# Two transformer blocks on one core: three pads and one moved tile change where the tiles of the on-chip memory begin

## The chip, the core and the metric

The kernel runs on one core of a Trainium2 chip. The metric is device time in microseconds for one execution. The kernel before took 1553.38 us, the median of three runs (1552.86 to 1556.38). One further execution was profiled; its own time stands in the table below.

The engines are TensorE (PE; its weight loads are listed apart as PEld), VectorE (DVE), ScalarE (ACT), GpSimd (POOL) and SyncE (SP, which issues nearly all transfers here). They share one on-chip memory of 128 partitions. A tile takes the same range of byte addresses in each partition, so a tile is placed by one number, its byte offset within a partition.

## The reference

Everything is float32, with 512 tokens and a model width of 1024. Cut to what matters:

```
first_block(x):
  u = rmsnorm(h); u_ssm, q, k, v = split(u @ w_in)              # 1024 -> 2048
  y_ssm  = s5_branch(u_ssm)                                     # 32 groups, state 64, gelu, glu
  y_attn = stick_breaking_attention(q, k, v)                    # 8 heads of 64
  gates  = sigmoid(u @ w_gate + b_gate)                         # 1024 -> 2048
  h += (g_ssm * (y_ssm @ w_up_ssm) + g_attn * (y_attn @ w_up_attn)) @ w_out
  h += relu(rmsnorm(h) @ w_ff1)**2 @ w_ff2                      # 1024 -> 4096 -> 1024
  return rmsnorm(h)
second_block(x, p):
  h += gla_mixer(rms_norm(h))          # gated linear attention, 4 heads, chunks of 64 tokens
  h += (p[0] @ ple_proj[0]) * sigmoid(rms_norm(h) @ ple_gate[0])
  h += fox_mixer(rms_norm(h))          # causal softmax attention with forget gates, 16 heads of 64
  h += (p[1] @ ple_proj[1]) * sigmoid(rms_norm(h) @ ple_gate[1])
  return rms_norm(h)
```

## The kernel before, in words

Activations stand with the features on the partitions and the 512 tokens along the free axis; `h` has 8 such chunks. Weights come as 105 units of 128 x 2048 floats (1 MB). SP loads a unit into one of two slots of `wraw`. ACT copies it, rounded, into `whi` (line 1044) and DVE writes the rest, `wraw - whi`, into `wlo` (line 1596). The activations are split in the same way: `uhi`/`ulo` (the normalised input), `yhi`/`ylo` and `ahi`/`alo` (the outputs of the two branches), `mhi`/`mlo` (the merged branches), `hdhi`/`hdlo` (the squared hidden layer), `pehi`/`pelo` (the `p` input).

The helper `three` (lines 498 to 500) makes each product from three matmuls, high x high, low x high and high x low. The profile names the operand that streams through the array (the moving one) first and the one that is loaded as weights (the stationary one) second: `ps<-uhi,whi` streams 512 columns of `uhi` past a 128 x 128 block of `whi`.

```
def three(out, lh, ll, rh, rl_, start, stop=False, done=None):
    nc.tensor.matmul(out, lh, rh, start=start, stop=False, skip_group_check=True)
    nc.tensor.matmul(out, lh, rl_, start=False, stop=False, skip_group_check=True)
    mm = nc.tensor.matmul(out, ll, rh, start=False, stop=stop, skip_group_check=True)
```

The stages, in the order of the program, with the stretch of the trace in which each lies:

- 0 to 264 us: first norm, then four rounds of `mixer`, each an S5 group and two heads of stick-breaking attention, with parts of the `w_in` products put between them. Small fp32 matmuls and transposes read `ident`, `ET`, `uch`, `Es`, `U4`, `M`, `H`, `X`; the attention reads `qs`, `kh`, `kl`, `athi`, `atlo`, `vhi`, `vlo`.
- 264 to 440 us: `merge`: the glu and the two up-projections (`y` and `a` tiles), the gates (`u`), and the output product (`m`).
- 440 to 800 us: `ff`, eight times: 96 matmuls on `u` (first layer), then 96 on `hd` (second layer), all with 512 columns.
- 800 to 1042 us: `gla_head` four times (its values are made with the weights streaming, `ps<-whi,uhi 128x256`), gates, output product.
- 1042 to 1150 us: `p[0]` product (`pe` tiles), its gate on `u`, norm.
- 1150 to 1430 us: `fox`, eight times two heads: scores from `fka`, `fkb`, `fq`, transposes of `pr`, values from `pthi`, `ptlo`, `fvhi`, `fvlo`, with `u` products between.
- 1430 to 1557 us: output product, `p[1]` product, gate, last norm.

The order of the work is written out by hand on each engine and is held by semaphores. No scheduler and no pool stands behind it. Tiles are placed by the stack of scopes at the head of `build` (lines 125 to 280): `sb` takes the next free bytes, rounded up to 32, and leaving a scope gives them back. So the offset of a tile is the sum of what stands before it. `vecs` has 97 floats (388 bytes, 416 with rounding), and `ident`, the tile behind it, therefore begins at a remainder of 32 when its offset is divided by 512.

These are the remainders modulo 512 of the tiles' offsets in the two built programs. Nearly every tile that TensorE reads has a length that is a multiple of 512 bytes, so the blocks within a tile mostly keep its remainder. Of the tiles near the top of the memory, `mlo` begins at byte 210784 before, `pthi` at 215936.

| tiles that TensorE reads | where read | before | after |
|---|---|---|---|
| `whi`, `wlo`, `uhi`, `ulo` | everywhere | 128 | 128 |
| `ident`, `ones`, `headones`, `identr`, `trir`, masks | norms, transposes, attention | 32 | 128 |
| `uch`, `vT`, `ET`, `H`, `Es`, `M`, `X`, `U4`, `tT` | S5, as fp32 | 96 | 128 |
| `qs`, `kh`, `kl`, `athi`, `atlo`, `vhi`, `vlo` | first attention | 96 | 128 |
| `acc`, `pp`, `pehi`, `pelo` | norms, `p` products | 96 | 128 |
| `yhi`, `ylo`, `ahi`, `alo`, `mhi`, `mlo` | merge | 352 | 128 |
| `hdhi`, `hdlo` | feed-forward | 352 | 128 |
| GLA tiles (`gr`, `kdec`, `qzhi`, `kihi`, `gvhi`, `aihi`, `sthi`, ...) | GLA | 352 | 128 |
| fox tiles (`fq`, `fka`, `fkb`, `fvhi`, `pr`, `pthi`, `ptlo`, ...) | fox | 384 | 128 |
| `rstd` (one column, broadcast) | norms | 128 | 224 |
| `wa2` | GLA, 8 matmuls | 224 | 320 |

Of the kernel before, what the change touches and what calls it, by code (L numbers as in the profile page):

```python
# [25 lines left out]
P = 128  # L26
# [9 lines left out]
GLA_N = 8  # L36
# [85 lines left out]
def build(nc, wstream, xT, pT, vecs_d, cst_d, s5p_d, wa2_d, outT):  # L122
    ctx = ExitStack()
    with ctx:
# [11 lines left out]
        whi = sb("whi", [P, 2, UW], F32R)  # L136
        wlo = sb("wlo", [P, 2, UW], F32R)
        vecs = sb("vecs", [P, NVEC])
        ident = sb("ident", [P, P])
        ones = sb("ones", [P, P])  # L140
        headones = sb("headones", [P, P])
# [19 lines left out]

        wa2 = sb("wa2", [16, T])
        s5r = sb("s5r", [P, 2, S5_PAIRS], F32R)

        with scope() as m:
            ys = sb("ys", [P, HC, T], F32, m)
            ya = sb("ya", [P, HC, T], F32, m)
            with scope() as e:
                blockpos = sb("blockpos", [P, NB], F32, e)
                s5p = sb("s5p", [P, 24, S5_PAIRS], F32, e)  # L170
                s5w = sb("s5w", [P, 5, 2, 2, S5_PAIRS], F32, e)
                s5b = sb("s5b", [P, 4, 512], F32, e)
                uch = sb("uch", [P, L, NB], F32, e)
                vT = sb("vT", [P, T], F32, e)
                ET = sb("ET", [P, 2, QP, L, 32], F32, e)
                H = sb("H", [P, 2, QP, L + 1, 32], F32, e)
                decay = sb("decay", [P, QP, NB], F32, e)
                with scope() as s:
                    sq = sb("sq", [P, 2, T], F32, s)
                    un = sb("un", [P, 2, T], F32, s)  # L180
                    acc = sb("acc", [P, T], F32, s)
                    with scope() as pl:
                        pe_in = sb("pe_in", [P, 2, T], F32, pl)
                        pehi = sb("pehi", [P, 2, T], F32R, pl)
                        pelo = sb("pelo", [P, 2, T], F32R, pl)
                        pp = sb("pp", [P, DC, T], F32, pl)
                        sg = sb("sg", [P, 2, T], F32, pl)

                    sq2, acc2 = un, pp[:, 6, :]
                    cst_in = sb("cst_in", [P, 5, P], F32, s)  # L190
                with scope() as s:
                    qs = sb("qs", [P, 2, T], F32R, s)
                    kh = sb("kh", [P, 2, T], F32R, s)
                    atlo = sb("atlo", [P, NZ], F32R, s)
                    vhi = sb("vhi", [P, TT, P], F32R, s)
                    vlo = sb("vlo", [P, TT, P], F32R, s)
                    att = sb("att", [P, NZ], F32, s)
                    athi = sb("athi", [P, NZ], F32R, s)
                    Es = sb("Es", [P, 2, 512], F32, s)
                    kl = sb("kl", [P, 2, T], F32R, s)  # L200
                    tmp = sb("tmp", [P, QP, L + 1, 32], F32, s)
                    M = sb("M", [P, QP, P], F32, s)
                    cosT = sb("cosT", [P, QP, NB], F32, s)
                    sinT = sb("sinT", [P, QP, NB], F32, s)
                    rin = sb("rin", [P, 2, QP, NB], F32, s)
                    zst = sb("zst", [P, 2, QP, NB], F32, s)
                    X = sb("X", [P, 2, QP, NB], F32, s)
                    U4 = sb("U4", [P, QP, NB], F32, s)
                    tT = sb("tT", [P, QP, P], F32, s)
                    gl = Es  # L210
            with scope() as s:
                yhi = sb("yhi", [P, HC, T], F32R, s)
                ylo = sb("ylo", [P, HC, T], F32R, s)
                ahi = sb("ahi", [P, HC, T], F32R, s)
                alo = sb("alo", [P, HC, T], F32R, s)
                gate = sb("gate", [P, 2, 4, T], F32, s)
                glu = sb("glu", [P, 2, T], F32, s)
                mg = glu
                mhi = sb("mhi", [P, DC, T], F32R, s)
                mlo = sb("mlo", [P, DC, T], F32R, s)  # L220
# [5 lines left out]
        with scope() as m:  # L226
            og = sb("og", [P, DC, T], F32, m)
            gr = sb("gr", [P, DC, T], F32, m)
            with scope() as s:
                alr = sb("alr", [P, T], F32, s)  # L230
                cum = sb("cum", [P, GLA_H, T], F32, s)
                eq = sb("eq", [P, T], F32, s)
                ek = sb("ek", [P, T], F32, s)
                kd = sb("kd", [P, T], F32, s)
                qin = sb("qin", [P, T], F32, s)
                kin = sb("kin", [P, T], F32, s)
                kdec = sb("kdec", [P, T], F32, s)

                qzhi = sb("qzhi", [P, TT, 4, GLA_C], F32R, s)
                qzlo = sb("qzlo", [P, TT, 4, GLA_C], F32R, s)  # L240
                kihi = sb("kihi", [P, T], F32R, s)
                kilo = sb("kilo", [P, T], F32R, s)
                kdhi = sb("kdhi", [P, T], F32R, s)
                kdlo = sb("kdlo", [P, T], F32R, s)
                gvhi = sb("gvhi", [P, TT, 256], F32R, s)
                gvlo = sb("gvlo", [P, TT, 256], F32R, s)
                ai = sb("ai", [P, TT, P], F32, s)
                aihi = sb("aihi", [P, TT, P], F32R, s)
                ailo = sb("ailo", [P, TT, P], F32R, s)
                st = sb("st", [P, 2, 256], F32, s)  # L250
                sthi = sb("sthi", [P, GLA_N, 256], F32R, s)
                stlo = sb("stlo", [P, GLA_N, 256], F32R, s)

                otm = gr[:, 4:6, :].rearrange("p a t -> p (a t)").rearrange("p (t c) -> p t c", c=256)
                gsq = gr[:, 6, 0:256]
                gss, g_half, g_t, g_y = (sb(n, [P, TT], F32, s) for n in ("gss", "g_half", "g_t", "g_y"))
            with scope() as s:
                fl = sb("fl", [16, 3, T], F32, s)
                nchi = sb("nchi", [16, T], F32R, s)
                nclo = sb("nclo", [16, T], F32R, s)  # L260
                gq8 = sb("gq8", [P, 1], F32, s)
                qk = sb("qk", [P, 2, T], F32, s)
                qksq = sb("qksq", [P, 2, T], F32, s)
                f_t = sb("f_t", [P, 2, T], F32, s)
                f_half = sb("f_half", [P, 2, T], F32, s)
                f_y = sb("f_y", [P, 2, T], F32, s)
                fq = sb("fq", [P, 2, 2, T], F32R, s)
                fka = sb("fka", [P, 2, T], F32R, s)
                fkb = sb("fkb", [P, 2, T], F32R, s)
                fvT = sb("fvT", [P, T], F32, s)  # L270
                fvhi = sb("fvhi", [P, TT, P], F32R, s)
                fvlo = sb("fvlo", [P, TT, P], F32R, s)
                pr = sb("pr", [P, NZ], F32, s)
                pthi = sb("pthi", [P, NZ], F32R, s)
                ptlo = sb("ptlo", [P, NZ], F32R, s)
                nmax = sb("nmax", [P, TT], F32, s)
                rsum = sb("rsum", [P, TT], F32, s)
                rinv = sb("rinv", [P, TT], F32, s)
        ps = ctx.enter_context(nc.psum_tensor("ps", [P, 8, 512], F32))
        flat = ps[:, :, :].rearrange("p b n -> p (b n)")  # L280

# [213 lines left out]
        def _(pe):  # L495
# [326 lines left out]
            def gla_head(i, last=False):  # L822
# [28 lines left out]
                for t in range(TT):  # L851
                    out = ps[:, 6 + t // 2, (t % 2) * 256:(t % 2) * 256 + 256]
                    three(out, aihi[:, t, :], ailo[:, t, :], gvhi[:, t, :], gvlo[:, t, :], True)
                    for v in range(2):
                        c = 2 * t + v
                        if c == 0:
                            continue
                        pe.wait_ge(st_ready, i * (GLA_N - 1) + c)
                        half = [q[:, t, 2 * v:2 * v + 2, :].rearrange("p a b -> p (a b)") for q in (qzhi, qzlo)]
                        three(out, *half, sthi[:, c, :], stlo[:, c, :], False, v == 1, go_mm if v == 1 and t % 2 else None)  # L860

                if not last:
                    gla_values(i + 1)
# [175 lines left out]
        def _(act):  # L1039
# [300 lines left out]
            def gla_head(i, last=False):  # L1340
# [6 lines left out]
                copy(aihi[:, :, :], ai[:, :, :]).then_inc(ai_hi, 1)  # L1347
                for c in range(GLA_N - 1):
                    act.wait_ge(st_done, i * (GLA_N - 1) + (c + 1))
                    copy(sthi[:, c + 1, :], st[:, c % 2, :]).then_inc(st_hi, 1)  # L1350
                if not last:
                    split_hi(None, U_GLA % 2, i + (U_GLA + 4) // 2, i * 4 + (DONE[U_GLA] + 6))

# [236 lines left out]
        def _(dve):  # L1590
# [435 lines left out]
            def gla_head(i, last=False):  # L2026
# [12 lines left out]
                for c in range(NS):  # L2039
# [7 lines left out]
                        V.scalar_tensor_tensor(st[:, c % 2, :], st[:, (c - 1) % 2, :], eq[:, at:at + 1], kv, ALU.mult,  # L2047
                                               ALU.add).then_inc(st_done, 1)
                    dve.wait_ge(st_hi, i * NS + (c + 1))
                    V.tensor_tensor(stlo[:, c + 1, :], st[:, c % 2, :], sthi[:, c + 1, :], ALU.subtract).then_inc(st_ready, 1)  # L2050
                    dve.wait_ge(st_ready, i * NS + (c + 1))
                split_lo(i * 2 + (U_GLA + 3), (U_GLA + 3) % 2)
                if not last:
# [375 lines left out]
```

## Time and profile before

| | |
|---|---|
| median of three runs | 1553.38 us |
| the profiled execution | 1558.66 us, of which the span from first to last instruction is 1556.9 us |
| mean granted TensorE clock | 0.963 of full speed |
| PE busy | 1433.3 us (92%) in 6912 matmuls |
| DVE busy, ACT busy, POOL busy | 949.2, 712.2, 81.8 us |
| DMA | 118.16 MB, 76 GB/s on average |
| chain that ended last | PE 68%, DVE 16%, ACT 11%, issue 5% |

How to read it: matmuls are pipelined, so the length of one record (about 0.4 us for 512 columns) is not what one costs. What a matmul costs in a dense row of them is the distance from its start to the next one's start. The rows of the timeline give starts to a hundredth of a microsecond, so that distance is taken over many matmuls: the difference of two starts, divided by how many matmuls lie between. In a run of `three` the lines 498, 499 and 500 repeat in that order, three matmuls for each line 499.

### The profile page before, as it was taken

Reading aid. Unit: us, or ns where it says so; the run is one execution under the profiler, and the core shown is the slowest. Engines: PE = TensorE matmul, PEld = TensorE weight load, DVE = VectorE, ACT = ScalarE, POOL = GpSimd, SP = SyncE. Lnnn points to the kernel's source line nnn. Section 1 sums busy time; section 2 is a strip of 40 time slices with the busy share of each in tenths; the row PEclk is TensorE's granted clock in tenths of the full one; section 3 lists DMA queues with packets and bytes.
Section 4 is the critical chain, followed back from the end, with each engine's and each line's share of the span. In section 5 each row is a group of like instructions: output and inputs, shape, how many; then the busy total and the mean of one; then the engine's idle time right before and its main releaser. Section 6 shows DMA issues by size and latency. Waiting matters only on the chain.

```text
span 1556.9 us, 18015 instructions
## 1 busy us (share of the span) xinstructions
PE 1433.3 (92%) x6912; PEld 1193.2 (77%) x6912; DVE 949.2 (61%) x1324; ACT 712.2 (46%) x940; POOL 81.8 (5%) x81
## 2 busy tenths in 40 slices
PE   4798889999989999999979999999789999996996
PEld 3687777788868888888868898787667777775875
DVE  6798776444354444444479676536776667777365
ACT  4577767332232222222246443334375666556251
POOL 3000000000200000000020000031100000000202
PEclk9999999999989999999989999999799999996998
DMA  5111011322212322222321122223121111111211
GB/s 188 55 54 55 1 55 54 109 90 99 98 65 81 108 84 104 90 99 81 108 82 55 54 85 76 96 81 109 55 81 54 54 54 54 54 54 68 81 55 54
DMA packets 19237, 118.16 MB, mean 76 GB/s; under 512 B 2400, under 2 KB 3680, under 8 KB 5616
## 3 DMA queue, kind: packets, MB, share of 16 engines
q1 hardware_dynamic: 18896, 116.38, 20.9%
q0 software_dynamic: 288, 1.05, 0.2%
q8 instruction: 37, 0.61, 0.2%
q14 instruction: 16, 0.13, 0.0%
HBM read 115.32 MB, written 2.10 MB: 75 GB/s over the span
## 4 chain that ended last, share of the span: by engine, by line
PE 68%; DVE 16%; ACT 11%; issue 5%; DVEq 0%; DMA 0%; ACTq 0%
PE ps L498 21%; PE ps L499 20%; PE ps L500 20%; DVE wlo L1596 1%; PE ps L681 1%; ACT whi L1044 1%; PE ps L951 1%; ACT fq L1044 1%; ACT fka L1044 1%; PE ps L562 1%; DVE att L1841 1%; DVE nmax L2164 1%; DVE acc L374 1%; ACT pthi L1044 1%; ACT att L1163 1%
## 5 line engine op out<-in xcount | busy, mean ns | idle before, releaser
L498 PE MATMUL ps<-uhi,whi 128*128 128x512 f32 x1168 | 469.2, 402 | 12.7 <-DVE ulo L1645 5.9
L499 PE MATMUL ps<-ulo,whi 128*128 128x512 f32 x1168 | 460.0, 394 | 0.0
L500 PE MATMUL ps<-uhi,wlo 128*128 128x512 f32 x1168 | 459.6, 393 | 0.0
L1596 DVE TENSOR_TENSOR wlo<-wraw,whi 128x2048 fp32r<-128x2048 f32 x105 | 240.2, 2290 | 109.8 <-ACT whi L1044 108.3
L1044 ACT ACTIVATE whi<-wraw 128x2048 fp32r<-128x2048 f32 x105 | 200.3, 1908 | 189.2 <-PE ps L500 189.0
L498 PEld LDWEIGHTS ps<-uhi,whi 128*128 128x128 f32 x1168 | 222.7, 191 | 66.5 <-issue 16.3
L500 PEld LDWEIGHTS ps<-uhi,wlo 128*128 128x128 f32 x1168 | 222.4, 190 | 47.8
L499 PEld LDWEIGHTS ps<-ulo,whi 128*128 128x128 f32 x1168 | 223.0, 191 | 45.9 <-issue 1.9
L498 PE MATMUL ps<-hdhi,whi 128*128 128x512 f32 x256 | 101.3, 396 | 0.0
L499 PE MATMUL ps<-hdlo,whi 128*128 128x512 f32 x256 | 101.3, 396 | 0.0
L500 PE MATMUL ps<-hdhi,wlo 128*128 128x512 f32 x256 | 101.2, 396 | 0.0
L1960 DVE TENSOR_TENSOR h<-ps,h 128x512 f32<-128x512 f32 x64 | 44.1, 690 | 54.7 <-PE ps L500 54.5
L1952 DVE TENSOR_TENSOR hd<-rl 128x512 f32<-128x512 f32 x32 | 22.0, 690 | 86.3 <-ACT rl L1287 86.3
L1287 ACT ACTIVATE rl<-ps 128x512 f32<-128x512 f32 x32 | 19.2, 599 | 118.0 <-PE ps L500 117.3
L2186 DVE TENSOR_TENSOR ptlo<-ps,pthi 128x1280 fp32r<-128x1280 f32 x16 | 23.9, 1491 | 63.8 <-ACT pthi L1044 63.8
L500 PEld LDWEIGHTS ps<-hdhi,wlo 128*128 128x128 f32 x256 | 48.1, 188 | 11.7
L499 PEld LDWEIGHTS ps<-hdlo,whi 128*128 128x128 f32 x256 | 48.1, 188 | 11.6
L498 PEld LDWEIGHTS ps<-hdhi,whi 128*128 128x128 f32 x256 | 48.1, 188 | 11.6
L1934 DVE TENSOR_TENSOR h<-ps,h 128x512 f32<-128x512 f32 x24 | 16.6, 691 | 65.0 <-PE ps L500 65.0
L1044 ACT ACTIVATE uhi<-un 128x512 fp32r<-128x512 f32 x48 | 30.1, 632 | 52.9 <-DVE un L1652 52.5
L1065 ACT ACTIVATE sq<-h 128x512 f32<-128x512 f32 x56 | 33.2, 621 | 41.6 <-DVE h L1934 24.2
L1480 ACT ACTIVATE pr<-ps,nmax 128x512 f32<-128x512 f32 (+1 forms) x64 | 32.9, 527 | 39.6 <-DVE nmax L2164 39.6
(391 smaller groups left out, 2371.5 us busy)
## 6 DMA issues: line engine op xcount, KB each, us to landing
wraw<-wstream SPq DMA_DIRECT2D x105, 1024.0 KB, 4.7
h<-xT SPq DMA_DIRECT2D x4, 512.0 KB, 5.6
outT<-pp SPq DMA_DIRECT2D x8, 256.0 KB, 2.1
s5b<-s5p_d SPq DMA_DIRECT2D x1, 1024.0 KB, 11.8
pe_in<-pT POOLq DMA_DIRECT2D x2, 512.0 KB, 3.7
cst_in<-cst_d SPq DMA_DIRECT2D x5, 64.0 KB, 10.1
reset<-cst_d SPq DMA_DIRECT2D x1, 256.0 KB, 11.1
ones<-cst_d SPq DMA_DIRECT2D x1, 64.0 KB, 2.2
```

The source lines that it names most:

```text
L498: nc.tensor.matmul(out, lh, rh, start=start, stop=False, skip_group_check=True)
L499: nc.tensor.matmul(out, lh, rl_, start=False, stop=False, skip_group_check=True)
L500: mm = nc.tensor.matmul(out, ll, rh, start=False, stop=stop, skip_group_check=True)
L1044: return A(out, in_, ACT.Copy, scale=scale)
L1065: A(sq[:, c % 2, :], h[:, c, :], ACT.Square).then_inc(sq_done, 1)
L1287: A(rl[:, m % 2, :], ps[:, a + m, :], ACT.Relu).then_inc(rl_done, 1)
L1480: e = A(pr[:, at], zf[:, at], ACT.Exp, bias=nmax[:, col], accum_out=rsum[:, col])
L1596: V.tensor_tensor(wlo[:, slot, :], wraw[:, slot, :], whi[:, slot, :], ALU.subtract).then_inc(lo_done, 1)
L1934: V.tensor_tensor(h[:, m, :], ps[:, banks[b] + k, :], h[:, m, :], ALU.add).then_inc(h_added, 1)
L1952: V.tensor_tensor(hd[:, m % 2, :], rl[:, m % 2, :], rl[:, m % 2, :], ALU.mult).then_inc(hd_done, 1)
L1960: V.tensor_tensor(h[:, m, :], ps[:, bank, :], h[:, m, :], ALU.add).then_inc(h_added, 1)
L2186: V.tensor_tensor(ptlo[:, :], tf, pthi[:, :], ALU.subtract).then_inc(pt_ready, 1)
```

## The change

It touches the placement of tiles, and for two of them the size. Two tiles named `pad0` (96 bytes) and `pad1` (192 bytes) are put in, which nothing reads or writes. `s5w` (1280 bytes, used by POOL and DVE in the set-up of the S5 part) moves from the scope `e` to the end of the scope behind `tT`. `gq8` (4 bytes, a factor used by DVE) moves to the end of its scope. `sthi` and `stlo` lose their first block of 256 columns, which no instruction used, and the indices into them go down by one. "Three pads" of the change's title are these two and the room that `gq8` took as one.

No instruction is added, removed or moved on any engine: the order of both programs is the same on PE, DVE, ACT, POOL and SP, and so are all semaphores, waits and transfers. Only addresses differ. `rstd` and `wa2` are read by TensorE and do not end up at 128 (table above).

```diff
         vecs = sb("vecs", [P, NVEC])
+        sb("pad0", [P, 24])
         ident = sb("ident", [P, P])
...
         s5r = sb("s5r", [P, 2, S5_PAIRS], F32R)
+        sb("pad1", [P, 48])
...
                 s5p = sb("s5p", [P, 24, S5_PAIRS], F32, e)
-                s5w = sb("s5w", [P, 5, 2, 2, S5_PAIRS], F32, e)
                 s5b = sb("s5b", [P, 4, 512], F32, e)
...
                     tT = sb("tT", [P, QP, P], F32, s)
+                    s5w = sb("s5w", [P, 5, 2, 2, S5_PAIRS], F32, s)
...
-                sthi = sb("sthi", [P, GLA_N, 256], F32R, s)
-                stlo = sb("stlo", [P, GLA_N, 256], F32R, s)
+                sthi = sb("sthi", [P, GLA_N - 1, 256], F32R, s)
+                stlo = sb("stlo", [P, GLA_N - 1, 256], F32R, s)
...
-                gq8 = sb("gq8", [P, 1], F32, s)
                 qk = sb("qk", [P, 2, T], F32, s)
...
                 rinv = sb("rinv", [P, TT], F32, s)
+                gq8 = sb("gq8", [P, 1], F32, s)
```

## Rows read from the trace of the kernel before

**Rows 1.** The page: chain that ended last, share of the span by engine.

```profile
PE 68%; DVE 16%; ACT 11%; issue 5%; DVEq 0%; DMA 0%; ACTq 0%
```

**Rows 2.** Busy time by stretch (us), four stretches; after PEclk the DMA share.

```profile
464.00:800.00 336.00, 334.65 (x1453) 272.52 (x1452) 154.62 (x158) 96.88 (x103) 6.16 (x5) 1.00 0.27 97
...
264.00:440.00 176.00, 170.13 (x736) 138.54 (x736) 73.14 (x82) 56.69 (x60) 11.94 (x6) 0.98 0.26 90
440.00:464.00 24.00, 21.68 (x86) 17.58 (x86) 16.77 (x23) 9.70 (x14) 0.00 (x0) 0.84 0.15 47
```

**Rows 3.** Timeline of PE, `hd` matmuls: start us, us, instruction.

```profile
688.64 0.40 PE L499 MATMUL ps<-hdlo,whi 128*128 128x512 f32 x1
...
709.64 0.40 PE L499 MATMUL ps<-hdlo,whi 128*128 128x512 f32 x1
```

**Rows 4.** Timeline of PE, the `u` matmuls behind them.

```profile
710.11 0.39 PE L498 MATMUL ps<-uhi,whi 128*128 128x512 f32 x1
...
711.72 0.39 PE L499 MATMUL ps<-ulo,whi 128*128 128x512 f32 x1
...
731.44 0.39 PE L499 MATMUL ps<-ulo,whi 128*128 128x512 f32 x1
```

**Rows 5.** Timeline of PE, the `m` and the `pe` matmuls.

```profile
387.11 0.40 PE L499 MATMUL ps<-mlo,whi 128*128 128x512 f32 x1
...
431.21 0.40 PE L499 MATMUL ps<-mlo,whi 128*128 128x512 f32 x1
...
1042.54 0.40 PE L499 MATMUL ps<-pelo,whi 128*128 128x512 f32 x1
...
1046.04 0.40 PE L499 MATMUL ps<-pelo,whi 128*128 128x512 f32 x1
```

**Rows 6.** Timeline of PE in fox and mixer: `u`, then value matmuls.

```profile
1200.29 0.39 PE L499 MATMUL ps<-ulo,whi 128*128 128x512 f32 x1
...
1205.55 0.39 PE L498 MATMUL ps<-pthi,fvhi 128*128 128x512 f32 x1
...
1206.23 0.33 PE L498 MATMUL ps<-pthi,fvhi 128*128 128x384 f32 x1
...
81.74 0.39 PE L498 MATMUL ps<-athi,vhi 128*128 128x512 f32 x1
...
82.43 0.34 PE L498 MATMUL ps<-athi,vhi 128*128 128x384 f32 x1
```

**Rows 7.** Groups by line and shape: matmuls; busy us, mean ns, idle before.

```profile
L498 PE MATMUL ps<-hdhi,whi 128*128 128x512 f32 x256 | 101.3, 396 | 0.0
...
L500 PE MATMUL ps<-mhi,wlo 128*128 128x512 f32 x64 | 25.3, 396 | 0.0
...
L498 PE MATMUL ps<-yhi,whi 128*128 128x512 f32 x48 | 19.1, 399 | 2.5 <-DVE ylo L1889 1.6 <-issue 0.8
...
L498 PE MATMUL ps<-pehi,whi 128*128 128x512 f32 x32 | 13.0, 406 | 0.0
...
L498 PE MATMUL ps<-ahi,whi 128*128 128x512 f32 x32 | 12.7, 396 | 0.0
...
L620 PE MATMUL ps<-U,Es 128*128 128x128 f32 x64 | 7.8, 275 | 0.0
```

**Rows 8.** Groups by line and shape: DVE and ACT on `u` and `hd` tiles.

```profile
L1645 DVE TENSOR_TENSOR ulo<-un,uhi 128x512 fp32r<-128x512 f32 x48 | 33.3, 693 | 3.5 <-ACT uhi L1044 2.8
...
L1956 DVE TENSOR_TENSOR hdlo<-hd,hdhi 128x512 fp32r<-128x512 f32 x32 | 20.7, 689 | 26.0 <-ACT hdhi L1044 26.0
```

**Rows 9.** Timeline of PE: 16 S5 matmuls, 8 transposes, and the start of `ff`.

```profile
65.85 1.95 PE L620 MATMUL ps<-U,Es 128*128 128x128 f32 x16
...
879.35 1.03 PE L870 MATMUL ps<-ident,gr 128*128 128x128 f32 x8
...
443.26 0.63 PE L499 MATMUL ps<-ulo,whi 128*128 128x512 f32 x1
443.69 0.63 PE L500 MATMUL ps<-uhi,wlo 128*128 128x512 f32 x1
```

More of the change, by code:

```diff
@@ L859, in gla_head @@
                         half = [q[:, t, 2 * v:2 * v + 2, :].rearrange("p a b -> p (a b)") for q in (qzhi, qzlo)]
-                        three(out, *half, sthi[:, c, :], stlo[:, c, :], False, v == 1, go_mm if v == 1 and t % 2 else None)
+                        three(out, *half, sthi[:, c - 1, :], stlo[:, c - 1, :], False, v == 1, go_mm if v == 1 and t % 2 else None)
                 if not last:
@@ L1349, in gla_head @@
                     act.wait_ge(st_done, i * (GLA_N - 1) + (c + 1))
-                    copy(sthi[:, c + 1, :], st[:, c % 2, :]).then_inc(st_hi, 1)
+                    copy(sthi[:, c, :], st[:, c % 2, :]).then_inc(st_hi, 1)
                 if not last:
@@ L2049, in gla_head @@
                     dve.wait_ge(st_hi, i * NS + (c + 1))
-                    V.tensor_tensor(stlo[:, c + 1, :], st[:, c % 2, :], sthi[:, c + 1, :], ALU.subtract).then_inc(st_ready, 1)
+                    V.tensor_tensor(stlo[:, c, :], st[:, c % 2, :], sthi[:, c, :], ALU.subtract).then_inc(st_ready, 1)
                     dve.wait_ge(st_ready, i * NS + (c + 1))
```

## The prediction

> **What bounds the kernel now.** I read the page first: PE carries 68% of the chain that ended last, DVE 16% of it and ACT 11% [rows 1]. Then the busy time by stretch: over the feed-forward stage, 464 to 800 us, PE is busy for 334.65 of 336.00 us while DVE is at 154.62 and ACT at 96.88; from 264 to 440 us it is 170.13 of 176.00 [rows 2]. So in those stretches the time is the number of matmuls times what one costs in a dense row, and nothing else.
>
> The change moves no instruction and no wait. It can act only through what an access costs at another address. So I then read, on the timeline, the distance between the starts of neighbouring matmuls of one shape (512 columns, full clock), family by family, and set it beside the table of offsets:
>
> - moving tile at 128, weights at 128 (`u` on `whi`): from 711.72 to 731.44 us lie 87 matmuls, so 19.72 / 87 = 226.7 ns each [rows 4].
> - moving tile at 352, weights at 128 (`hd`): from 688.64 to 709.64 us lie 90 matmuls, so 21.00 / 90 = 233.3 ns [rows 3]. The `m` tiles, also at 352: 44.10 / 189 = 233.3 ns. The `pe` tiles, at 96: 3.50 / 15 = 233.3 ns [rows 5]. The `y` and `a` tiles are at 352 too; I take the same for them.
> - both at 384 (`pthi` on `fvhi`): 0.68 / 3 = 226.7 ns. Both at 96 (`athi` on `vhi`): 0.69 / 3 = 230 ns, three matmuls only [rows 6].
>
> So the cheaper spacing goes with 128 and 384, the dearer one with 96 or 352, or with operands that differ. These data do not separate "both operands at one remainder" from "each on a multiple of 64 bytes" (128 and 384 are, 96 and 352 are not), and they need not: after the change all these tiles are at 128, which satisfies both. Other causes I looked for do not fit. `m` has `u`'s shape, 8 chunks, and still costs 233.3; `pthi` lies as high in the memory as `mlo` and costs 226.7; `hd` and `u` alternate in one stage beside the same DVE, ACT and DMA work.
>
> **The change, part by part.** Each row family that goes from 233.3 to 226.7 ns gains 6.67 ns a matmul. The counts are three times those of one line in the groups [rows 7].
>
> - `hd`: 3 x 256 = 768 matmuls x 6.67 ns = 5.1 us. All on the path: PE never stops there, and DVE and ACT are idle for half of the stage and more [rows 2].
> - `m`: 3 x 64 = 192, 1.3 us. On the path: a dense row, and the norm behind it waits for its last block.
> - `y` and `a`: 3 x (48 + 32) = 240, 1.6 us. On the path by the same stretch of 264 to 440 us, where PE is idle for 5.9 us in all.
> - `pe`: 3 x 32 = 96, 0.6 us. They stand in program order ahead of the matmuls that spread the norm, so I count them whole. If DVE's norm scale came later than they end, up to 0.6 us would be hidden.
>
> Together 1296 matmuls and 8.6 us. The rest is small or unknown:
>
> - Starts of a row. Behind `hd`, the first seven spacings of `u` take 1.61 us, 230 ns each, before 226.7 sets in [rows 4]: 0.02 us. With one remainder everywhere I expect this to go at the 8 passages of the feed-forward stage, 0.2 us. In fox, 23 spacings from 1200.29 to 1205.55 us average 228.7 ns [rows 6], 0.05 us above 226.7; there are about 48 such short rows of 24 in fox and mixer, 2.2 us if all of it went. But these start behind shorter matmuls, whose lengths do not change, and fox's tiles (384) already have the cheap spacing. Nearest to the first kind, I take 0.4 us in all, bounds 0 and 2.4.
> - Matmuls of 128 columns. Sixteen of S5 (`U`, `Es`, both at 96) take 1.95 us, of which the last record is 0.275 [rows 7], so (1.95 - 0.275) / 15 = 112 ns each; eight transposes (`ident` at 32, `gr` at 352), with a last record as long, take (1.03 - 0.275) / 7 = 108 ns [rows 9]. The one matched pair is the slower one. Either it is the kind of instruction, and nothing changes, or equal remainders cost 4 ns here: all transposes by `ident` (336 in the program, by its loops) would then lose 1.3 us. If instead S5's 160 gain 3 ns, that is 0.5 us. I take 0, bounds 0.5 gained and 1.3 lost.
> - DVE and ACT. The same subtraction costs 693 ns with its tiles at 96 and 128 and 689 ns at 352 [rows 8]. So their times do not follow the offset: 0. The dearest bound that these rows allow is 4 ns on the 32 `hdlo`, 0.1 us, hidden under PE.
> - `s5w`, `gq8`, `sthi`, `stlo`: same instructions, a few kilobytes elsewhere, 0. `rstd` and `wa2`, which leave their remainder, feed 64 and 8 matmuls; even 7 ns on each is 0.5 us.
>
> Sum: 8.6 + 0.4 = 9.0 us off the profiled execution, 1558.66 to 1549.7. The median of the runs is 5.3 us below that execution; the difference should be the same there: 1553.38 - 9.0 = 1544.4 us, 0.58% faster.
>
> The `hd` row shows the gain at TensorE with the granted clock at 1.00, the 2.4 GHz level. By the Trainium skill, "TensorE: Matmul & The Clock Gate", Part 2, the array streams one column per cycle, a 512-column matmul follows the last after about 216 ns, and TensorE has two independent read ports, so loading the next weights takes nothing from the running matmul. By that rule the offset would mean nothing, and the sum would be 0. The trace does not agree: it has 226.7 and 233.3 ns [rows 3, 4], both above 216, and which one follows the tile.
>
> **The rivals.**
>
> - No change. The spacing follows something that goes along with the tiles and not their offset, such as the region of the memory, and the two kinds stay as they are. For it: the data are five families, not an experiment. Against it: `m` with `u`'s shape, and `mlo` and `pthi` in one region with different spacings. It gives 1553.4 us. The Trainium skill's rule above would end here, and so would "SBUF — State Buffer", the box on cachelines, which charges only for steps across lines of 16 bytes: all these offsets are multiples of 32.
> - Part of it given back. PE is faster and a wait takes over: the second layer's weights or the sums `h` are not ready, or the norm scale holds the `pe` rows. For it: in 264 to 440 us PE does wait 5.9 us already. Against it: DVE has 181 us free in the stage of 336 us that holds 5.1 us of the gain. If only the `hd` half of the terms came, 1553.4 - 5.1 + 1.3 for dearer transposes = 1549.6 us.
> - More than the sum. The starts of rows gain their 2.4 us in full and S5 its 0.5: 8.6 + 2.4 + 0.5 = 11.5, 1541.9 us.
> - Slower. Behind each norm, PE restarts at a granted clock of 0.5 (1.2 GHz): at 443 us a matmul takes 0.43 us [rows 9], and the stretch 440 to 464 us has 0.84 [rows 2]. When the clock returns is not tied to the program, so a program whose stretches shift by some microseconds can meet it worse. Each matmul more at the low level costs 0.43 - 0.23 = 0.20 us. From 45 more of them the gain of 9.0 us is gone, from 61 the kernel is over 0.2% slower; at 65 it is 1553.4 - 9.0 + 13.0 = 1557.4 us. Against it: the granted clock falls at the waits for norms, which do not change, and the three runs of before, with whatever they met, span 3.5 us, which is 18 such matmuls.
>
> **How the numbers follow.** The sum as worked out: 0.72, with a range of its own of 1542 to 1547 us (8.6 less the 0.6 that may be hidden and the 1.3 of the transposes, at the one end; the whole of the starts of rows, 11.0, at the other). More than the sum: 0.09. Part given back: 0.09. No change: 0.07. Slower: 0.03. Without the last two the terms span 1541.9 to 1549.6; with 1.4 us, under half of the 3.5 us that the three runs span, added on the fast side, and the upper end left there, the range is 1540.5 to 1549.6 us.
>
> What a measurement of this kernel can tell from no change is about 0.2%, 3.1 us. The sum, the larger one, and most of the partial case lie beyond it: faster 0.87. Same: the case of no change and a little of the partial one, 0.10. Slower 0.03.
>
> **What would show it.** In the profile after: `hd`, `m`, `y`, `a` and `pe` rows at 226.7 ns; the record of an `hd` matmul at 0.39 us in place of 0.40, like that of `u` [rows 3, 4]; a feed-forward stage (464 to 800) shorter by 5.1 to 5.3 us, with PE still without waits; 264 to 440 us shorter by 2.9. `u` rows without the seven dearer spacings behind `hd`. Transposes by `ident` at 108 ns: if they are at 112, the term of 1.3 us applies. DVE and ACT groups unchanged. The prediction is wrong if `hd` stays at 233.3 ns, if `u` rises above 226.7, or if the stages are shorter as said and the total is not: then the time went into waits or the clock, which the busy time by stretch shows.

## The result, and the profile after

| | before | after |
|---|---|---|
| median of 7 runs | 1556.38 us (1552.86 to 1557.77) | 1546.09 us (1539.76 to 1550.05) |
| the profiled execution | 1558.66 us | 1539.76 us, the fastest of its runs |
| mean granted TensorE clock in it | 0.963 | 0.973 |

The ratio of the runs is 0.9935 with a 95% interval of 0.9913 to 0.9958: 10.1 us faster (6.5 to 13.5). A second comparison, further down, gave 0.9931 (0.9916 to 0.9946). The forecast was 1544.4 us in a range of 1540.5 to 1549.6. The three runs of before that the forecast started from lay low: over 7, 10 and 16 runs its median came out at 1556.4, 1556.0 and 1553.5.

The timeline of PE in the kernel after, at the places of [rows 3 to 5] (the lines of `three` are now 500 to 502): a row of `hd`, the row of `u` behind it, `m`, `pe`.

```profile
677.75 0.39 PE L501 MATMUL ps<-hdlo,whi 128*128 128x512 f32 x1
...
698.15 0.39 PE L501 MATMUL ps<-hdlo,whi 128*128 128x512 f32 x1
...
698.60 0.39 PE L500 MATMUL ps<-uhi,whi 128*128 128x512 f32 x1
698.83 0.39 PE L501 MATMUL ps<-ulo,whi 128*128 128x512 f32 x1
...
719.91 0.39 PE L501 MATMUL ps<-ulo,whi 128*128 128x512 f32 x1
...
382.27 0.39 PE L501 MATMUL ps<-mlo,whi 128*128 128x512 f32 x1
...
425.11 0.39 PE L501 MATMUL ps<-mlo,whi 128*128 128x512 f32 x1
...
1027.31 0.39 PE L501 MATMUL ps<-pelo,whi 128*128 128x512 f32 x1
...
1030.71 0.39 PE L501 MATMUL ps<-pelo,whi 128*128 128x512 f32 x1
```

`hd`: 20.40 us over 90 matmuls, 226.7 ns; before, 21.00 us over the same 90 [rows 3]. `m`: 42.84 over 189 in place of 44.10, and `pe`: 3.40 over 15 in place of 3.50 [rows 5], both 226.7 ns. From the last `hd` row to the first `ulo` and on through the 93 matmuls to 719.91 (21.08 us, 226.7 ns) no spacing is longer: the seven dearer ones at the start of [rows 4] are gone.

Groups of the kernel after, as in [rows 7 and 8]: busy us, mean ns of one | idle before.

```profile
L500 PE MATMUL ps<-hdhi,whi 128*128 128x512 f32 x256 | 99.6, 389 | 0.0
...
L500 PE MATMUL ps<-ahi,whi 128*128 128x512 f32 x32 | 12.4, 389 | 0.0
...
L1647 DVE TENSOR_TENSOR ulo<-un,uhi 128x512 fp32r<-128x512 f32 x48 | 33.3, 694 | 3.5 <-ACT uhi L1046 2.8
...
L1958 DVE TENSOR_TENSOR hdlo<-hd,hdhi 128x512 fp32r<-128x512 f32 x32 | 20.7, 689 | 26.0 <-ACT hdhi L1046 26.0
```

A record of an `hd` or `a` matmul is 7 ns shorter (389 for 396). DVE takes what it took: 694 and 689 ns against 693 and 689, now that `hdlo` stands at 128.

The stretches of [rows 2], shifted to the same work: us, PE busy, PEld, DVE, ACT, POOL, granted clock, DMA share, GB/s.

```profile
261.10:433.40 172.30, 166.84 (x736) 137.73 (x736) 73.05 (x81) 56.33 (x59) 11.92 (x6) 0.99 0.26 92
```

The 736 matmuls from the first `y` row to the norm take 172.30 us, PE busy for 166.84 of them; before, 176.0 and 170.13. PE stopped for 5.5 us, before for 5.9: nothing of the gain went into waits here. These 3.7 us are more than the 2.9 of the forecast. The rows themselves give 2.7: from the first to the last `yhi` matmul, all at full clock, it is 119.40 us before and 117.96 after, and the `m` row has the 1.26 us above. The rest goes with the granted clock, 0.99 in place of 0.98 (4.5 us at half clock in this stretch in place of 6.2). First and last `yhi` matmul, before:

```profile
264.44 0.47 PE L498 MATMUL ps<-yhi,whi 128*128 128x512 f32 x1 [1.64 <-DVE ylo L1889]
...
383.84 0.40 PE L500 MATMUL ps<-yhi,wlo 128*128 128x512 f32 x1
```

After:

```profile
261.14 0.47 PE L500 MATMUL ps<-yhi,whi 128*128 128x512 f32 x1 [1.67 <-DVE ylo L1891]
...
379.10 0.39 PE L502 MATMUL ps<-yhi,wlo 128*128 128x512 f32 x1
```

### The profile page after: what moved, and what is told of

The parts are those of the page before. It is cut to its first block, busy times and chain, and to the rows that moved or that the text cites. A ratio compares the mean times of both kernels' runs of the same rounds, so it can differ in the third digit from the quotient of the medians.

```text
span 1538.0 us, 18015 instructions
## 1 busy us (share of the span) xinstructions
PE 1412.2 (92%) x6912; PEld 1182.8 (77%) x6912; DVE 949.0 (62%) x1324; ACT 711.9 (46%) x940; POOL 81.7 (5%) x81
## 4 chain that ended last, share of the span: by engine, by line
PE 64%; DVE 17%; ACT 12%; issue 6%; DVEq 0%; DMA 0%; ACTq 0%
PE ps L500 20%; PE ps L502 19%; PE ps L501 19%; DVE wlo L1598 2%; ACT whi L1046 1%; PE ps L683 1%; ACT fq L1046 1%; PE ps L953 1%; ACT fka L1046 1%; DVE acc L376 1%; DVE att L1843 1%; DVE nmax L2166 1%; PE ps L564 1%; ACT pthi L1046 1%; ACT att L1165 1%
## 5 line engine op out<-in xcount | busy, mean ns | idle before, releaser
L501 PEld LDWEIGHTS ps<-hdlo,whi 128*128 128x128 f32 x256 | 48.0, 188 | 10.1
## 6 DMA issues: line engine op xcount, KB each, us to landing
cst_in<-cst_d SPq DMA_DIRECT2D x5, 64.0 KB, 10.2
```

## The experiments

There are ten experiments. Nine move tiles (the first two also leave out one unused constant tile and the copy that fills it); the tenth is the changed kernel once more. Each was read the same way: starts of 512-column matmuls of one family, at full clock, far enough from the start of the row. "Distance" is the offset of the moving tile less that of the stationary one, in bytes and modulo 512. A tile's `hi` and `lo` parts have the same remainder.

**1. One remainder for all, but not a multiple of 64.** All tiles shifted by 224 bytes. To make room, the constant tile `onesr`, which nothing reads, and the copy that fills it are left out.

```diff
+        sb("padg", [P, 56])
         h = sb("h", [P, DC, T])
-        onesr = sb("onesr", [P, P], F32R)
```

> Every tile that TensorE reads, weights included, begins at 352 modulo 512; one unused constant tile and its copy are left out. Theory 'match' (a matmul is cheap when moving and stationary operand have one remainder modulo 512): all 512-column rows at 226.7 ns, time as after, about 1546 us. Theory 'own' (each operand has to begin on a multiple of 64 bytes; 352 does not): all 4800 matmuls with 512 columns at 233.3 ns, 30 us more than after, about 1575 us.

Measured 1544.22 us, one run. Timeline, `hd`, then `u`:

```profile
464.75 0.39 PE L501 MATMUL ps<-hdlo,whi 128*128 128x512 f32 x1
...
484.47 0.39 PE L501 MATMUL ps<-hdlo,whi 128*128 128x512 f32 x1
...
487.19 0.39 PE L501 MATMUL ps<-ulo,whi 128*128 128x512 f32 x1
...
505.55 0.39 PE L501 MATMUL ps<-ulo,whi 128*128 128x512 f32 x1
```

19.72 / 87 and 18.36 / 81: both 226.7 ns with every tile at 352. The theory that each operand needs its own alignment to 64 bytes falls. What counts is how the two stand to each other.

**2. The weights alone moved.** The kernel before, with `wraw`, `whi`, `wlo` at 352; `onesr` and its copy are left out again.

```diff
+        sb("padw", [P, 56])
         wraw = sb("wraw", [P, 2, UW])
...
+        sb("padv", [P, 72])
         vecs = sb("vecs", [P, NVEC])
```

> The kernel before with the weight tiles alone moved from 128 to 352; u stays at 128, hd, m, y and a at 352, pe at 96. 'match': hd, m, y, a at 226.7 ns, u and pe at 233.3: 8 us gained and 22 lost, about 1569 us against 1555. 'own': every 512-column row at 233.3 ns, about 1577 us, as whi itself is off a multiple of 64.

Measured 1565.14 us, one run, against 1553.49 for one run of before on that chip. Timeline, `hd`, `u`, `pe`:

```profile
469.88 0.39 PE L500 MATMUL ps<-hdlo,whi 128*128 128x512 f32 x1
...
488.24 0.39 PE L500 MATMUL ps<-hdlo,whi 128*128 128x512 f32 x1
...
491.01 0.40 PE L500 MATMUL ps<-ulo,whi 128*128 128x512 f32 x1
...
509.91 0.39 PE L500 MATMUL ps<-ulo,whi 128*128 128x512 f32 x1
...
1047.78 0.39 PE L500 MATMUL ps<-pelo,whi 128*128 128x512 f32 x1
...
1049.82 0.39 PE L500 MATMUL ps<-pelo,whi 128*128 128x512 f32 x1
```

The roles change over: `hd`, untouched at 352, now has 226.7 ns (18.36 / 81), and `u`, untouched at 128, has 233.3 (18.90 / 81). So it is no property of a tile, its data or its own place alone. The expectation was about 1569 us: the run is 11.7 us above before in place of 14, and the spacings added up below give 11.5 (22.8 against 11.3). One detail goes against both expectations: `pe`, at 96 and so 256 bytes from the weights, has 226.7 ns too (2.04 / 9). The modulus is then at most 256.

**3. Other distances.** The changed kernel with pads ahead of `mhi`, `hdhi`, `pehi` (and one behind `pelo` that restores what follows). Of the three kernels the first had pads of 64, 32 and 8 floats, the second 24, 16 and 64, the third 48, 40 and 16.

```diff
+                sb("pad3", [P, 64], F32, s)
                 mhi = sb("mhi", [P, DC, T], F32R, s)
...
+            sb("pad4", [P, 32], F32, s)
             hdhi = sb("hdhi", [P, 4, T], F32R, s)
...
+                        sb("pad5", [P, 8], F32, pl)
                         pehi = sb("pehi", [P, 2, T], F32R, pl)
```

> The changed kernel with three families moved off again: m at 384 (256 from the weights), hd at 256 (128 from them), pe at 160 (32 from them). 'match' modulo 512: all three at 233.3 ns, 7 us more than after. 'own', or a match modulo 64 only: m and hd stay at 226.7, pe at 233.3, 0.6 us more than after. A match modulo 256: m 226.7, hd 233.3.

> The changed kernel with m at 224 (96 from the weights), hd at 192 (64 from them), pe at 384 (256 from them). 'match' modulo 512: all three at 233.3 ns. 'own' or a match modulo 64: hd and pe at 226.7, m at 233.3. A match modulo 128: hd at 233.3 as well.

> The changed kernel with m 192 bytes, hd 160 and pe 64 from the weights. If the cost depends on the distance modulo 256 alone and is the same to both sides: m (192, that is -64) at 229.1 ns like hd at +64, hd (160, that is -96) at 233.3, pe (64) at 229.1. If the side matters: m at another value than 229.1.

They took 1554.24, 1549.21 and 1555.97 us, one run each. Timeline of the first of them, `m` and `hd`:

```profile
388.01 0.39 PE L505 MATMUL ps<-mlo,whi 128*128 128x512 f32 x1
...
407.73 0.39 PE L505 MATMUL ps<-mlo,whi 128*128 128x512 f32 x1
...
464.69 0.40 PE L505 MATMUL ps<-hdlo,whi 128*128 128x512 f32 x1
...
485.00 0.39 PE L505 MATMUL ps<-hdlo,whi 128*128 128x512 f32 x1
```

`m` at distance 256: 19.72 / 87 = 226.7 ns. `hd` at 128: 20.31 / 87 = 233.4 ns. The second kernel's `hd`, at distance 64, and the third's `hd`, at 160, and `m`, at 192:

```profile
465.94 0.39 PE L505 MATMUL ps<-hdlo,whi 128*128 128x512 f32 x1
...
484.48 0.39 PE L505 MATMUL ps<-hdlo,whi 128*128 128x512 f32 x1
```

```profile
465.70 0.40 PE L505 MATMUL ps<-hdlo,whi 128*128 128x512 f32 x1
...
485.38 0.40 PE L505 MATMUL ps<-hdlo,whi 128*128 128x512 f32 x1
...
387.91 0.39 PE L505 MATMUL ps<-mlo,whi 128*128 128x512 f32 x1
...
407.51 0.39 PE L505 MATMUL ps<-mlo,whi 128*128 128x512 f32 x1
```

18.54 / 81 = 228.9 ns, 19.68 / 84 = 234.3 ns and 19.60 / 84 = 233.3 ns. All the readings together, now with 288 and 480 (`u` in experiment 2, `pe` before) written modulo 256, as 32 and 224:

| distance | 0 | 256 | 64 | 32 | 96 | 128 | 160 | 192 | 224 |
|---|---|---|---|---|---|---|---|---|---|
| ns a matmul | 226.7 | 226.7 | 229 | 233.3 | 233.4 | 233.4 | 234.3 | 233.3 | 233.3 |
| families | all | `m`, `pe` | `hd`, `pe` | `pe`, `u` | `m` | `hd` | `hd` | `m` | `hd`, `m`, `pe` |

In the first kernel the last of the three cases came, a match modulo 256. In the second none came as written, for `hd` at distance 64 lies between the two levels. The modulus is 256, not 512 and not 64 or 128. In the third, `m` shows that it is not the same to both sides: 64 ahead costs 2 ns, 64 behind (192) costs 6.7.

**4. Distances under 32 bytes.** The changed kernel with views that begin 4 (`hd`), 2 (`m`) and 1 (`pe`) floats into tiles 8 floats wider, and pads that hold the tiles themselves at 128.

```diff
-            hdhi = sb("hdhi", [P, 4, T], F32R, s)
+            hdhi = sb("hdhi", [P, 4 * T + 8], F32R, s)[:, 4:4 + 4 * T].rearrange("p (a t) -> p a t", t=T)
```

> The changed kernel with hd 16 bytes, m 8 bytes and pe 4 bytes behind the weights' remainder. If the cost starts with any distance: 227 to 233 ns for each. If it works in steps of 16 bytes or more: m and pe at 226.7. If some distance is better than none: under 226.7 ns.

Measured 1555.15 us, one run. Timeline, `hd` (16 bytes) and `pe` (4 bytes):

```profile
466.76 0.40 PE L505 MATMUL ps<-hdlo,whi 128*128 128x512 f32 x1
...
486.92 0.40 PE L505 MATMUL ps<-hdlo,whi 128*128 128x512 f32 x1
...
1041.90 0.40 PE L505 MATMUL ps<-pelo,whi 128*128 128x512 f32 x1
...
1044.04 0.40 PE L505 MATMUL ps<-pelo,whi 128*128 128x512 f32 x1
```

20.16 / 87 = 231.7 ns at 16 bytes, 2.14 / 9 = 237.8 ns at 4; `m` at 8 bytes had 19.52 / 84 = 232.4. Even one float costs, the most of all, and more than the 233 ns that I had put as the upper end. No distance tried is better than none. Whether below 32 bytes it is the distance, or the operand's own start off a multiple of 16 or 32 bytes, stays open: the weights were not moved along.

**5. One part alone, and all but that part.** `hd` moved to 128 in the kernel before (a pad of 72 floats ahead of `hdhi`), and `hd` put back to 352 in the changed kernel (56 floats).

```diff
+            sb("pad4", [P, 72], F32, s)
             hdhi = sb("hdhi", [P, 4, T], F32R, s)
```

> The kernel before with one pad, which moves only hd from 352 to 128. Theory 'the whole gain on the path': hd at 226.7 ns, the stretch from the first to the eighth hd row shorter by 4.6 us, and 5.1 to 5.3 us less than before in the runs, if the clock falls alike. Rival 'given back': hd at 226.7 ns, but waits in the stage and under 2 us less in all. All other spacings as before.

> The changed kernel with only hd put back to 352. Theory 'two terms' (the time is the spacings over 226.7 ns plus about 0.30 us for each us at half clock, and the half-clock time behind the feed-forward stage depends on that stage's length): hd at 233.3 ns, 5.3 us more spacing than in the changed kernel, half clock between 790 and 900 us for 17 us or more instead of 13.7, about 1552 us in the median, 6 to 8 us slower than the changed kernel. Theory 'spacing alone, clock by chance': 5.3 us slower than the changed kernel, 1550.9 us, and the half-clock time of that stretch 13.7 us as often as not.

`hd` at 128 alone: 1546.79 us (6 runs) against 1556.02, ratio 0.9951 (0.9933 to 0.9968). All but `hd`: 1550.10 us (11 runs) against 1553.52, ratio 0.9978 (0.9966 to 0.9990). The first and last start of the 256 `hdlo` matmuls, in the order before, after, `hd` alone, all but `hd`:

```profile
L499 PE MATMUL ps<-hdlo,whi x256: 395/396/397, 467.0 to 798.0; 128*128 128x512 f32 x128
```

```profile
L501 PE MATMUL ps<-hdlo,whi x256: 389/389/389, 459.5 to 785.2; 128*128 128x512 f32 x128
```

```profile
L500 PE MATMUL ps<-hdlo,whi x256: 389/389/389, 463.0 to 788.7; 128*128 128x512 f32 x128
```

```profile
L502 PE MATMUL ps<-hdlo,whi x256: 395/396/397, 459.9 to 791.0; 128*128 128x512 f32 x128
```

331.0, 325.7, 325.7 and 331.1 us: the stage gets 5.3 us shorter with `hd` at 128 whatever the rest does, 5.1 from `hd` and, as the difference, 0.2 from the starts of the `u` rows. "Given back" falls here. The totals do not part the expectations as well. `hd` alone is 9.2 us below before in the medians where 5.1 to 5.3 were expected, at a mean clock of 0.9693 beside 0.9660. All but `hd` is 3.4 us below before, as its spacings say. It ran on another chip than the changed kernel, so 1550.10 us does not decide between the 1550.9 of "spacing alone" and the 1552 of "two terms"; its half-clock time between 790 and 900 us was 20.5 us, as "two terms" has it, but see below.

**6. The changed kernel again.**

> The changed kernel once more, timed in five rounds, to part the spacing from the clock. If the spacing is all, it is 8.7 us faster than before at an equal mean granted clock. If the shorter half-clock time of the profiled run belongs to the change, its mean granted clock is above that of before in nearly every run, and it is 15 us or more faster.

1545.55 us (6 runs) against 1556.02, ratio 0.9931 (0.9916 to 0.9946): 10.7 us. That is between the two cases. Its mean clock is 0.967 to 0.971, that of before on the same chip 0.964 to 0.969: higher in the mean (0.9690 and 0.9660), but not in nearly every run.

**7. A smaller edit.** From the changed kernel: `pad0` cut to 8 floats, `pad1` left out, `s5w` back in its place.

```diff
-        sb("pad0", [P, 24])
+        sb("pad0", [P, 8])
...
-        sb("pad1", [P, 48])
```

> One pad of 32 bytes in place of pads of 96 and 192, s5w back in its place: y, a, m, hd and the fox and GLA tiles at 384, weights and u at 128, ident at 64. Theory 'distance modulo 256': all 512-column rows at 226.7 ns, 1545.6 us like the changed kernel within 0.2%. Theory 'modulo 512': y, a, m and hd at 233.3 ns, 8 us slower than the changed kernel.

1547.26 us (6 runs) against 1553.52, ratio 0.9953 (0.9936 to 0.9970). Timeline, `hd` at 384 on weights at 128:

```profile
463.16 0.39 PE L500 MATMUL ps<-hdlo,whi 128*128 128x512 f32 x1
...
482.88 0.39 PE L500 MATMUL ps<-hdlo,whi 128*128 128x512 f32 x1
```

19.72 / 87 = 226.7 ns. One pad of 32 bytes, with the moved `gq8` and the shorter `sthi` and `stlo`, gives the same spacings in the large rows, and a time within 0.2% of the changed kernel's, as expected. The two were timed on different chips, 6.3 us below before on one and 10.5 on the other; the comparison at equal clock below finds no difference between them.

**The clock.** Adding up the spacing over 226.7 ns of all 512-column matmuls at full clock gives 11.3 us for before and 2.6 for after. Against the profiled difference of 18.9 us that leaves 10.2. The records of the granted clock have it at half for 116 us of the span before and 82 after. Over twelve profiles:

| kernel | spacing over 226.7 ns, us | half clock, us | span, us |
|---|---|---|---|
| before | 11.3 | 116 | 1556.9 |
| after, first and second profile | 2.6, 2.6 | 82, 102 | 1538.0, 1545.1 |
| all at 352 | 2.6 | 92 | 1542.4 |
| weights at 352 | 22.8 | 105 | 1563.4 |
| other distances, three kernels | 8.2, 6.0, 9.9 | 112, 99, 106 | 1552.4, 1547.4, 1554.2 |
| under 32 bytes | 8.6 | 106 | 1553.4 |
| `hd` alone, all but `hd` | 6.1, 7.9 | 95, 99 | 1544.3, 1548.4 |
| smaller edit | 2.1 | 102 | 1544.4 |

Span = 1511.6 us + the spacing + 0.297 x the half-clock time, its two constants fitted to these twelve, meets them all within 2.4 us; by it the 34 us less at half clock are the 10.2. A least-squares fit over the runs (27 of before, 13 of after, 6, 11 and 6 of the last three kernels) with the mean clock as a term gives, at equal clock: after 7.2 us below before (standard error 0.4), `hd` alone 4.6 (0.5), all but `hd` 3.4 (0.4), the smaller edit 7.3 (0.5). Each 0.001 of mean clock is worth 0.96 us.

## Why the prediction was right, point by point

- The level of the spacings. All four terms came as worked out. Added up from the starts: `hd` 5.13 us of excess gone (5.1 forecast), `m` 1.27 (1.3), `y` and `a` 1.49 (1.6), `pe` 0.48 (0.6); the last two families keep a few dear spacings behind stops. Together 8.4 of the 8.6 us.
- All of it on the path: nearly. In stretches that ran at full clock both times, `hd` and the starts behind it took 5.3 us less (331.0 and 325.7 us, and the undone part), `y`, `a` and `m` 2.7 less. Of `pe`, part was hidden, as the forecast allowed: from its first matmul to the first `u` behind it, it is 13.75 and 13.57 us for `p[0]`, 13.77 and 13.60 for `p[1]`, so 0.35 of 0.48 us came through. That is 8.4 us in all.
- Starts of rows. Forecast 0.4, measured 0.2, as forecast for the 8 passages of the feed-forward stage alone. The row of fox that stood in [rows 6] takes 5.24 us where it took 5.26: its dear start stays, although all its tiles now have one remainder.
- Matmuls of 128 columns, `DVE` and `ACT`: 0, as taken. The eight transposes by `ident` take 1.04 us with operands at one remainder, 1.03 before [rows 9], so the loss of 1.3 us that I bounded did not come. An S5 matmul takes 111 to 112 ns in both, but its operands have one remainder before and after, so it tests nothing. (By the groups of the profile S5 has 224 such matmuls, not 160.)

Two rows of the kernel after show it, the second with its mate of before in [rows 9]:

```profile
1183.01 0.39 PE L501 MATMUL ps<-ulo,whi 128*128 128x512 f32 x1
...
1188.25 0.39 PE L500 MATMUL ps<-pthi,fvhi 128*128 128x512 f32 x1
...
865.65 1.04 PE L872 MATMUL ps<-ident,gr 128*128 128x128 f32 x8
```

- The sum. Forecast 9.0 us. All spacings together give 8.7, of which the 8.4 above can be followed on the path; the medians of the two comparisons give 10.3 and 10.5. The amount on top goes with the clock: the mean granted clock over the runs is 0.9669 for before and 0.9689 for after, which at 0.96 us for 0.001 is 1.9 us. The forecast had the clock only as the rival that makes the kernel slower. It went the other way.
- The two ways of counting do not meet exactly. Over all runs the means differ by 9.2 us; the fit puts 1.9 of them down to the clock and leaves 7.2 at equal mean clock, give or take 0.8 at 95%. That is 1.2 below the 8.4 of the rows. The mean clock does not say whether PE had work while the clock was low, which may be the reason; that is not shown.
- The level. 1544.4 us was forecast, 1546.09 measured. The start of the sum lay 3.0 us low (1553.38 where seven runs have 1556.38), and the gain came out 1.3 us larger than forecast. That the two errors partly cancel is luck.
- The rival "no change" fell with the first profile. The Trainium skill's rule in "TensorE: Matmul & The Clock Gate", Part 2, that loading weights takes nothing from the running matmul, does not account for experiment 2, which changes 226.7 to 233.3 ns by the address of the weights alone.
- What I left open, one remainder or a multiple of 64 bytes, was settled for the first, but modulo 256. `pthi` on `fvhi`, both at 384, could not have told: their distance is 0.
- Why the distance costs time stays open. The loads of weights overlap the running matmuls (before, PEld is busy for 1193.2 us and PE for 1433.3 of 1556.9), and all blocks of `whi` and `wlo` have one remainder, so the runs do not even tell whether a matmul's own weights count or those that are loaded beside it for the next.

Does the change itself raise the clock? It is not shown. `hd` alone had 0.9693 over its 6 runs, beside 0.9660 for the runs of before on that chip, but the smaller edit, with the changed kernel's spacings, had 0.9675 beside 0.9674. My expectation that a long feed-forward stage brings more half clock behind it also fails on that kernel. The stretch 790 to 900 us, for after, all but `hd`, and the smaller edit (granted clock ahead of the DMA share):

```profile
790.00:900.00 110.00, 105.38 (x670) 93.27 (x671) 86.66 (x156) 52.11 (x80) 1.54 (x2) 0.94 0.18 67
```

```profile
790.00:900.00 110.00, 101.54 (x614) 88.68 (x613) 88.27 (x156) 54.83 (x84) 5.88 (x4) 0.91 0.21 77
```

```profile
790.00:900.00 110.00, 103.02 (x635) 90.89 (x636) 87.19 (x155) 52.64 (x79) 3.74 (x3) 0.91 0.18 67
```

0.94, 0.91, and 0.91 again although the third kernel's stage is as short as the first's. So the surplus of the medians goes with the clock, and why the clock was higher in those runs stays open.

## What to carry to other kernels

- Where TensorE bounds a kernel and each matmul loads its own weights, read the distance between starts in a dense row, tile by tile. Two families of one shape with different spacings point at addresses; here a difference of 6.7 ns in 1296 matmuls was 8.6 us.
- For matmuls of 512 columns, put moving and stationary tiles at the same byte offset modulo 256. One small tile between them is enough to spoil it, and one pad enough to mend it. Slices that begin a few floats into a tile spoil it too.
- Where the effect is half a per cent, compare runs with their mean clock beside them, and take the size of the effect from the starts in the timeline: the changed kernel's `hd` rows had 226.7 ns in both of its profiles, whose spans differ by 7 us.

## What the runs showed of the hardware that I had not expected

- The spacing depends on the distance modulo 256 and not evenly: 226.7 ns at 0, 229 at +64, 233.3 at -64, 234.3 at +160, 237.8 at +4 bytes (there with operands that begin off a multiple of 16 bytes as well).
- With 256 columns the sign is the other way. In GLA the weights stream past a block of `u`. At distance 0 (after) and with the weights 224 bytes off (experiment 2):

```profile
854.25 0.28 PE L501 MATMUL ps<-wlo,uhi 128*128 128x256 f32 x1
...
864.69 0.28 PE L501 MATMUL ps<-wlo,uhi 128*128 128x256 f32 x1
```

```profile
870.05 0.28 PE L500 MATMUL ps<-wlo,uhi 128*128 128x256 f32 x1
...
881.05 0.28 PE L500 MATMUL ps<-wlo,uhi 128*128 128x256 f32 x1
```

10.44 / 87 = 120.0 ns at one remainder, 11.00 / 93 = 118.3 ns off it. Over GLA's 384 such matmuls that is 0.6 us. It was not to be had here, since the same tiles meet with 512 columns elsewhere. One other distance was read, so no rule for 256 columns follows.
